# S5 in a hybrid diffusion trunk: inputs, in-chunk matrices, outputs and modulation rows as narrow matmuls in column tiles

## The reference, cut to what matters

```
mod = silu(cond) @ ada_w[l] + ada_b[l]            # 6 x 1024 numbers a layer, for each of the two token groups
sh1, sc1, g1, sh2, sc2, g2 = split(mod, 6)
h = rmsnorm(x, g) * (1 + sc1) + sh1
```

```
u = proj[..., 1536:].reshape(n_tok, 32, 16)
h[t] = lam_bar * h[t-1] + b_bar @ u[t]
y[t] = Re(c_mat @ h[t])                           # for each direction; the second runs over reversed tokens
y = gelu(y_f + y_b + d * u);  y = y * sigmoid(y @ glu_w + glu_b)
```

## Time and profile before

| | |
|---|---|
| median of 3 runs | 4515.22 us (4513.23 to 4517.06) |
| the profiled execution's own time | 4515.3 us |
| its span, first to last instruction | 4513.5 us |
| TensorE busy | 4206.5 us (93%) |
| VectorE busy | 2955.5 us (65%) |
| GpSimd busy | 1619.6 us (36%) |
| ScalarE busy | 751.1 us (17%) |

### The profile page before, as it was taken

The page is one execution under the profiler, slowest core; times in us unless marked ns, Lnnn a source line. Parts: engine busy times, 40 slices in busy tenths (PEclk is TensorE's granted clock), DMA queues, the critical chain, the costliest instruction groups (busy, mean ns, idle before and its releaser), DMA issues. The chain is left out here.

```text
span 4513.5 us, 44328 instructions
## 1 busy us (share of the span) xinstructions
PE 4206.5 (93%) x15630; PEld 2476.9 (55%) x15630; DVE 2955.5 (65%) x5889; ACT 751.1 (17%) x1583; POOL 1619.6 (36%) x1472
## 2 busy tenths in 40 slices
PE   7785669999999999999989997999999999999998
PEld 3552445768554555545536875576855455554553
DVE  5447953999876766557634227499987676664763
ACT  2121441037000000000002222102810000000000
POOL 1003300028566655545400000001956564554640
PEclk9897889999999999999999999999999999999999
DMA  4111641137999999979921204112789999997993
GB/s 166 52 58 39 228 182 58 56 107 223 364 357 365 410 360 365 353 293 410 350 86 56 70 28 91 41 57 85 223 338 363 366 410 360 363 361 287 406 359 119
DMA packets 354408, 1045.42 MB, mean 232 GB/s; under 512 B 31657, under 2 KB 132361, under 8 KB 343002
## 3 DMA queue, kind: packets, MB, share of 16 engines
q0 software_dynamic: 148096, 545.34, 31.7%
q1 hardware_dynamic: 107036, 447.12, 26.8%
q10 hardware_dynamic: 99072, 50.33, 4.0%
HBM read 988.54 MB, written 54.14 MB: 231 GB/s over the span
## 5 line engine op out<-in xcount | busy, mean ns | idle before, releaser
L592 PE MATMUL banks<-blocks,picked_T 128*128 128x512 f32 x3072 | 1359.1, 594 | 16.0 <-DVE picked_T L772 16.0
L555 PE MATMUL banks<-h_dense_T,blocks 128*128 128x384 f32 x4096 | 1357.6, 486 | 0.0
L555 PEld LDWEIGHTS banks<-h_dense_T,blocks 128*128 128x128 f32 x4096 | 776.9, 190 | 581.9 <-issue 98.5
L592 PEld LDWEIGHTS banks<-blocks,picked_T 128*128 128x128 f32 x3072 | 585.9, 191 | 711.6 <-issue 657.5
L383 POOL DMA_INDIRECT expert_rows<-in_pk_u_dram,expert x512 | 667.3, 1303 | 478.6 <-DVE own_dots L787 253.7
L383 POOL DMA_INDIRECT expert_rows<-in_pk_v_dram,expert x512 | 601.1, 1174 | 514.5 <-DVE acc L806 262.4
L806 DVE SCALAR_TENSOR_TENSOR acc<-expert_rows,expert_weight,acc 128x1024 f32<-128x1024 f32 x504 | 622.8, 1282 | 67.4 <-DMA expert_rows<-in_pk_v_dram,expert 66.8
L787 DVE CUSTOM_DVE_ANT_0 expert_rows<-expert_rows,h_rows 128x1024 f32<-128x1024 f32 x512 | 601.5, 1221 | 59.1 <-DMA expert_rows<-in_pk_u_dram,expert 57.6
L772 DVE TENSOR_TENSOR picked_T<-dense_act,shared 128x384 f32<-128x384 f32 x246 | 209.9, 854 | 569.6 <-PE banks L592 560.1
L408 ACT ACTIVATE dense_act<-banks 128x384 f32<-128x384 f32 x246 | 120.6, 490 | 2229.8 <-PE banks L555 2229.6
L374 POOL TENSOR_SCALAR expert_rows<-iota,picked_T 128x128 f32<-128x128 f32 x384 | 251.2, 672 | 472.7 <-ACT picked_T L414 415.9
(11 more groups left out here) (495 smaller groups left out, 3788.7 us busy)
## 6 DMA issues: line engine op xcount, KB each, us to landing
blocks<-in_pk_u_turned_dram SPq DMA_DIRECT2D x256, 512.0 KB, 6.6
blocks<-in_pk_v_dram SPq DMA_DIRECT2D x256, 512.0 KB, 6.7
gates_dram<-shared ACTq DMA_DIRECT2D x48, 1024.0 KB, 5.1
shared<-gates_dram SPq DMA_DIRECT2D x32, 1536.0 KB, 11.4
ada_block<-in_ada_rest_dram SPq DMA_DIRECT2D x32, 1280.0 KB, 7.5
blocks<-in_pk_w_q_dram SPq DMA_DIRECT2D x32, 512.0 KB, 3.4
MIXT<-in_ev_w_in_dram SPq DMA_DIRECT2D x16, 512.0 KB
expert_rows<-in_pk_u_dram,expert POOLq DMA_INDIRECT x512, 8.4
```

The source lines that it names most:

```text
L555: mm = pe.matmul(dense_dots(c), u[:, k * P:(k + 1) * P], HT[:, k, :], start=(k == 0), stop=(k == KD - 1))
L592: mm = pe.matmul(ps[:, at_:at_ + HALF], wt[:, c % WEIGHED, z * P:(z + 1) * P], v[:, half_ * HALF:(half_ + 1) * HALF], start=(c == 0), stop ...
```

## The change

- `even_inputs`: for the four S5 blocks `products` gives way to `chunk_products`. The weights of a block are taken 32 columns at a time, and for each of the four tokens j of a chunk one matmul streams HT at every fourth token and writes partitions 32 j to 32 j + 31. The product then lies as UP needs it, and one copy of 128 x 640 drains it.
- `s5`, `inside`: for each pair, the 32 columns of token j are made in partitions 32 j, 128 columns wide, so M lies in PSUM as it is used; one copy of 128 x 512 moves it. The diagonal is added by four small matmuls for each pair.
- `s5`, `outputs`: for each token j and pair i a matmul with 32 columns of M (and of CL) writes partitions 32 i; Gelu then takes two pieces of 128 x 320 and not 16 of 32 x 160.
- Modulation rows: cond_s becomes 32 columns wide, the last 30 zero, and so every quarter of the array writes 32 partitions. One copy moves all 128 partitions; two stores pick the two rows of each quarter out of it.
- Counts of the semaphores follow. cond_s is cleared at the start, and ScalarE waits for that; it now lives until the end of layer 0's mixer and not to the end of the program.

```
@@ even_inputs, tensor
+            def chunk_products(i, b):
+                pe.wait_ge(w_in[b], 16 * i + 16)
+                pe.wait_ge(x_out, 2 * i + (b - 1))
+                for n in range(4):
+                    at = (2 * b + n // 2) * HALF + n % 2 * CHUNKS
+                    for k in range(KD):
+                        lhs = w[:, b, k * P + 32 * n:k * P + 32 * n + 32]
+                        for j in range(T4):
+                            mm = pe.matmul(ps[32 * j:32 * j + 32, at:at + CHUNKS], lhs,
+                                           HT[:, k, j::T4], start=(k == 0), stop=(k == KD - 1))
+                mm.then_inc(used, 1)
...
             for b in range(2):
-                products(hyena // 2, b)
+                chunk_products(hyena // 2, b)
                 turn(hyena // 2 - 1, b)
             for b in range(2):
-                products(hyena // 2 + 1, b)
+                chunk_products(hyena // 2 + 1, b)
@@ even_inputs, scalar, drain_chunks
-                    "p (h t) -> p h t", h=2)[:, :, 0:EVEN]
-                for k in range(4):
-                    for j in range(T4):
-                        ins = act.activation(
-                            UP[32 * j:32 * j + 32, m, k, :].rearrange("p (h c) -> p h c", h=2),
-                            src[32 * k:32 * k + 32, :, j::T4], ACT.Copy)
-                ins.then_inc(x_out, 1)
+                    "p (h t) -> p h t", h=2)[:, :, 0:2 * CHUNKS]
+                act.activation(UP[:, m].rearrange("p (h k) c -> p h (k c)", h=2), src, ACT.Copy
+                               ).then_inc(x_out, 1)
@@ s5, sync, ada_store
-                sp.wait_ge(ada_copied, 4 * (n + 1))
-                sp.dma_start(mod[:, at:at + MOD_W], mod_now[:, b, :]).then_inc(mod_out[b], 16)
+                sp.wait_ge(ada_copied, n + 1)
+                for g in range(2):
+                    to = mod[g:g + 1, at:at + MOD_W].rearrange("g (j c) -> (g j) c", j=4)
+                    sp.dma_start(to, mod_now[g::32, b, :]).then_inc(mod_out[b], 16)
@@ s5, scalar
-                for j in range(4):
-                    act.activation(mod_now[:, b, ADA_COLS * j:ADA_COLS * (j + 1)],
-                                   ps[32 * j:32 * j + 2, ADA0:ADA0 + ADA_COLS], ACT.Copy
-                                   ).then_inc(ada_copied, 1)
+                act.activation(mod_now[:, b, :], ps[:, ADA0:ADA0 + ADA_COLS], ACT.Copy
+                               ).then_inc(ada_copied, 1)
...
-                for i in range(4):
-                    for j in range(T4):
-                        at = K0 + 32 * (3 - j)
-                        act.activation(M[32 * j:32 * j + 32, i, :], ps[32 * i:32 * i + 32, at:at + P],
-                                       ACT.Copy).then_inc(m_set, 1)
+                act.activation(M[:], ps[:, K0:K0 + HALF].rearrange("p (i c) -> p i c", c=P), ACT.Copy
+                               ).then_inc(m_set, 1)
...
-                for i in range(4):
-                    for j in range(T4):
-                        act.activation(G[32 * i:32 * i + 32, m, j::T4],
-                                       ps[32 * j:32 * j + 32, y_at(i):y_at(i) + CHUNKS],
-                                       ACT.Gelu_apprx_tanh).then_inc(y_out, 1)
+                to = G[:, m, :].rearrange("p (c j) -> p j c", j=T4)
+                for n in range(2):
+                    src = ps[:, y_at(2 * n):y_at(2 * n) + 2 * CHUNKS]
+                    act.activation(to[:, 2 * n:2 * n + 2, :], src.rearrange("p (j c) -> p j c", j=2),
+                                   ACT.Gelu_apprx_tanh).then_inc(y_out, 1)
@@ s5, tensor, ada_row
-                            mm = pe.matmul(ps[32 * j:32 * j + 2, ADA0:ADA0 + ADA_COLS],
+                            mm = pe.matmul(ps[32 * j:32 * j + 32, ADA0:ADA0 + ADA_COLS],
                                            cond_s[:, KD // 2 * h + k, :], ada[:, h, at:at + ADA_COLS],
                                            start=(h == 0 and k == 0), stop=False)
@@ s5, tensor, inside
-                for d in range(2):
-                    for part in range(2):
-                        for i in range(4):
-                            pe.matmul(ps[32 * i:32 * i + 32, K0:K0 + 224],
-                                      BL[:, m % 2, part, 4 * d + i, 3 - 3 * d, :],
-                                      CL[:, part, 4 * d + i, d:d + 7, :].rearrange("p s j -> p (s j)"),
-                                      start=(d == 0 and part == 0), stop=False)
                 for i in range(4):
-                    mm = pe.matmul(ps[32 * i:32 * i + 32, K0 + 96:K0 + 128],
-                                   ident[0:2 * S5C, 0:2 * S5C], diag[:, 4 * m + i, :],
-                                   start=False, stop=True)
+                    at = K0 + P * i
+                    for d in range(2):
+                        for part in range(2):
+                            for j in range(T4):
+                                first = d + T4 - 1 - j
+                                pe.matmul(ps[32 * j:32 * j + 32, at:at + P],
+                                          BL[:, m % 2, part, 4 * d + i, 3 - 3 * d, :],
+                                          CL[:, part, 4 * d + i, first:first + T4, :].rearrange(
+                                              "p s j -> p (s j)"),
+                                          start=(d == 0 and part == 0), stop=False)
+                    for j in range(T4):
+                        mm = pe.matmul(ps[32 * j:32 * j + 32, at + 32 * j:at + 32 * j + 32],
+                                       ident[0:2 * S5C, 0:2 * S5C], diag[:, 4 * m + i, :],
+                                       start=False, stop=True)
@@ s5, tensor, outputs
-                for i in range(4):
-                    at = y_at(i)
-                    pe.matmul(ps[:, at:at + CHUNKS], M[:, i, :], UP[:, m, i, :], start=True, stop=False)
+                for j in range(T4):
+                    at = y_at(j)
+                    for i in range(4):
+                        pe.matmul(ps[32 * i:32 * i + 32, at:at + CHUNKS], M[:, i, 32 * j:32 * j + 32],
+                                  UP[:, m, i, :], start=True, stop=False)
                     for d in range(2):
                         for part in range(2):
-                            mm = pe.matmul(
-                                ps[:, at:at + CHUNKS],
-                                CL[:, part, 4 * d + i, 4 - 4 * d:8 - 4 * d, :].rearrange(
-                                    "p s j -> p (s j)"),
-                                PREV[:, part, 4 * d + i, :], start=False, stop=(d == 1 and part == 1))
+                            for i in range(4):
+                                mm = pe.matmul(ps[32 * i:32 * i + 32, at:at + CHUNKS],
+                                               CL[:, part, 4 * d + i, 4 - 4 * d + j, :],
+                                               PREV[:, part, 4 * d + i, :], start=False,
+                                               stop=(d == 1 and part == 1))
@@ trunk
-        cond_s = buf(ctx, nc, "cond_s", [P, KD, 2])
...
+            cond_s = buf(c1, nc, "cond_s", [P, KD, 32])
```

More of the change, by code:

```diff
@@ L1014, in modulation @@
                         col = k * HALF + quarter * j
-                        pe.matmul(ps[32 * j:32 * j + 2, at:at + quarter], cond_s[:, k, :],
+                        pe.matmul(ps[32 * j:32 * j + 2, at:at + quarter], cond_s[:, k, 0:2],
                                   w[b % 2][:, col:col + quarter], start=(k == 0), stop=False)
@@ L1087, in _ @@
             act.wait_ge(cond_in, 16)
-            act.activation(cond_s[:], cond[:], ACT.Silu).then_inc(cond_ready, 1)
+            act.wait_ge(ones_set, 1)
+            act.activation(cond_s[:, :, 0:2], cond[:], ACT.Silu).then_inc(cond_ready, 1)
             act.wait_ge(decay_in, 16)
@@ L1138, in _ @@
             line = Line(dve, dve_line)
+            line.count(dve.memset(cond_s[:], 0.0))
             line.then(dve.memset(ones[:], 1.0))
@@ L1704, in s5 @@
         ada_b = buf(ctx, nc, "ada_bias", [1, 2, MOD_W])
-        mod_now = buf(ctx, nc, "mod_rows", [2, 2, MOD_W])
-        ones = buf(ctx, nc, "one_one", [1, 2])
+        mod_now = buf(ctx, nc, "mod_rows", [P, 2, ADA_COLS])
+        ones = buf(ctx, nc, "one_row", [1, 32])
         N = 2 * PAIRS
@@ L1782, in _ @@
             for b in range(2):
-                sp.wait_ge(mod_out[b], 16 * MOD_BLOCKS // 2)
+                sp.wait_ge(mod_out[b], 32 * MOD_BLOCKS // 2)
             for part, out in ((0, out_re), (1, out_im)):
@@ L1838, in ada_copy @@
                 if n >= 2:
-                    act.wait_ge(mod_out[b], 16 * (n // 2))
-                for j in range(4):
-                    act.activation(mod_now[:, b, ADA_COLS * j:ADA_COLS * (j + 1)],
-                                   ps[32 * j:32 * j + 2, ADA0:ADA0 + ADA_COLS], ACT.Copy
-                                   ).then_inc(ada_copied, 1)
+                    act.wait_ge(mod_out[b], 32 * (n // 2))
```

(17 more changed lines are left out.)

## The result

The changed kernel takes 4544.07 us (median of 4 runs, 4540.92 to 4548.34); the kernel before, beside it, 4516.14 (4513.23 to 4517.91). The ratio is 1.0063, 95% interval 1.0046 to 1.0081: slower by 28 us. The forecast was 4539. The profiled execution is the longest of the four: 4548.34 us, span 4546.5, so +33.0 on the span of before. I read it in the order of the prediction's steps.

A forecast was written before the change was run, and what follows sets the result against it. Bound: stages separated by barriers, TensorE then a ScalarE tail in the input projection, VectorE in S5. +35.1 - 2.8 - 2.7 - 5.9 = +23.7 on 4515.3 gave 4539 us; own range 4530 to 4552, wider 4497 to 4558.

The forecast's parts named there:

- Part 4: Even layer's input projection: TensorE streaming every fourth token takes 0.288 us a group, so the stage ends 35.1 us later.
- Part 5: Hyena's start: with shorter TensorE idle the clock stays up, first eight records 2.8 us less.
- Part 3: End of S5: 16 Gelu pieces on ScalarE become two, saving 5.9 us.
- Part 1: Modulation rows: wider weights' loads hidden, extra store and memset cost nothing; ScalarE copies 0.9 us less, 16 times.
- Part 2: S5's last pass: in-chunk matrix ready about 1 us earlier; with two modulation copies, VectorE's wait 2.7 us shorter.
- A: Rival: the input projection's streamed step is free or nearly so for TensorE; -15.2 us, 4500 us; chance 0.29.
- B: Rival: the input projection's four strips hinder each other; 4613 us in pairs, about 4760 all in turn; chance 0.10.
- C: Rival: TensorE's longer in-chunk matrix work becomes the bound of S5; 4542 us, only moving the forecast; no chance given.

The follow-up runs named there:

- the run with one stream: Changed kernel with the four S5 blocks by 128-column weights, 64 records of 160 columns a block, still streaming every fourth token; 4543.13 us (one run).
- the five buffers: HT by place with the modulation weights in five buffers of a quarter row instead of two of half a row; 4501.45 us, ratio 0.9972.
- HT by place: Changed kernel with HT stored by the token's place in its chunk, so records stream neighbouring words; ScalarE orders it copying from PSUM; 4508.40 us, ratio 0.9985.
- the kernel with its inputs put back: Changed kernel with the four S5 blocks back to 128-column matmuls and 16-piece copies; 4513.43 us, ratio 0.9997.

## Why the prediction was right, and where it was not

**Part 4, the inputs (+35.1), carried the result and was right in mechanism and size.** Groups of four records 0.290 us apart for 0.288, a block 18.59 for 18.4. That the stage's end, 342.65 us, meets the 342.7 to 0.05 is luck: the four blocks cost 39.7 us more and not 39.3, and the first began 0.5 us sooner. The row it was priced from, ScalarE writing at the same step, was the right one among three; an estimate from VectorE's row (0.75 ns a word more) would have been 0.256 us a group, and from the weight loads' (206 ns for 141) 0.199. Why the two engines fall by the same factor at this step, no run shows. The experiments add that the price belongs to a word alone in its 16 bytes (8 bytes: 5%; 32 bytes: 1% more than 16), whatever the tiles and the number of streams.

**Part 5, Hyena's start (-2.8): -3.5.** The clock stayed up. That a short idle time is enough for it was too simple, as the run with one stream shows.

**Part 3, the outputs (-5.9): -6.1.** A piece takes what was forecast or more (0.73 us forecast, 731 to 975 ns measured), but the last two overlap and are through in 1.29 us together, not 1.5. The line's eight pieces, ns of one as minimum, median and maximum:

```profile
L1901 ACT ACTIVATE US<-banks x8: 731/805/975, 538.5 to 666.3; 128x320 f32<-128x320 f32 x8
```

**Part 1 (nothing): right.** A row of 64 records takes 2.38 us with 32-column weights, 2.36 with 2.

**Part 2, the in-chunk matrices with two modulation copies (-2.7): wrong; the gain did not come.** The step that failed reads "That lies on the chain to VectorE's 5.19 us wait", by which all that ScalarE saves comes off the wait. What it puts ahead of that was sound: the block on TensorE fell inside its bounds (598.22 to 605.29 us, 7.1), and the matrix was ready 7.8 us after the block's start instead of 8.1. (Its bounds are wider than its own terms, which give 0.9 us later to 2.6 earlier, and with the two copies 0.8 to 4.3 off the wait.) ScalarE let TensorE go on with the turning 13.2 us after the block's start (598.22 to 611.40) instead of 14.7 (566.75 to 581.46): 1.5 won. But I followed ScalarE alone. Behind the turning TensorE needs the second half of a row's weights. Its load is issued only when the row before has freed the buffer, and the longer block stands ahead of that row: 9.9 us after the block's start (608.14) instead of 6.1 (572.88). Before, the 16 pieces gave it the time to land. Now TensorE waited 2.42 us for it, its clock fell, and line 1979's work took 7.56 us, where it takes 5.49 at the upper level (the five buffers). From that second half of the turning to the end of VectorE's wait it is 15.2 us instead of 12.8: 2.3 lost. In this pair of executions the wait grew by 0.8; over all of them it is no shorter. S5 as a whole is 6.6 us shorter, not 8.6.

**What the sum left out.** It took the 3868 us behind S5 as unchanged. They are 8 us longer in the profiled execution. By medians less: the time rose by 27.9 us, 24.9 of it by the start of the stage behind S5, which leaves 3. For +24 this is small; for the kernels that gain it is not: in the profiled executions HT by place loses 3.0 of 13.6 us there, and the kernel with its inputs put back 8.0 of 9.8.

**The rivals.** A (the step is free) needed a block near 8.7 us; only neighbouring words give that. B (strips in turns) falls with the run of one stream. C was right that TensorE's chain in the last pass ends S5's slack. It put the wait 0.5 us longer, near what was measured, but by records at the lower clock; the runs show the wait for weights beside them.

## What to carry to other kernels

Price a strided operand by what shares its 16 bytes, on the engine that streams it: TensorE's streams here went at half speed from 16 bytes on, and making the order once, in the copy out of PSUM, cost ScalarE nothing (615 ns for 613). When a slow step on one engine goes, look for the transfer that it had covered: its buffer comes free no sooner than before (here later), and the wait appears there. Before a wait of a few us is called longer or shorter, look at it in several executions: this one spread over 1.8 us under the same S5 code. And a gain of a few us ahead of a long TensorE part can be lost in it in part, in records at the lower clock at the starts of its stages; judge it by the time of the whole.

## What the runs showed of the hardware that was not expected

- A streamed fp32 operand: 0.139 us for a group of 160 columns at neighbouring words (8.90 / 64), 0.147 at 8 bytes, 0.290 at 16, 0.294 at 32; four streams abreast cost what one does.
- ScalarE reads PSUM one word in four at no price when it writes runs of 32 words: 615 ns for 512 columns, 613 in order.
- After 1.58 us of idle the granted clock was 1.00 behind narrow tiles streaming at 16 bytes, and after 1.54 us 0.50 behind full-width records at the same rate. In all eight kernels with the narrow tiles Hyena's first records ran at the upper level.
- What records at the clock's lower level cost behind S5 repeated to 0.2 us in two executions of one kernel of like length, and differs by up to 8 us between kernels that are alike in that part.
